# V rows of the second token half gathered as 32 tokens of four experts, multiplied in four column groups of TensorE

## What is computed

```python
def peer_ffn(xn, w_query, sub_keys, expert_u, expert_v):
    ...                       # q, scores, top 16 of each half, top 16 of the pairs
    expert_idx = jnp.take_along_axis(cand_i, best_pos, axis=-1)   # 8 x 16 experts per token
    gates = jax.nn.softmax(best_s, axis=-1)
    def chunk_fn(args):
        xb, ib, gb = args
        u = expert_u[ib]
        act = jax.nn.gelu(jnp.einsum('ced,cd->ce', u, xb))
        return jnp.einsum('ce,ced->cd', gb * act, expert_v[ib])
```

## Time and profile before

| | us |
|---|---|
| median of 3 runs | 2021.76 (2018.59 to 2022.65) |
| the profiled execution, its own time | 2023.32 |
| its span in the trace | 2021.6 |
| mean granted clock of TensorE | 0.97 |

### The profile page before, as it was taken

The page is one execution under the profiler, slowest core; times in us unless marked ns, Lnnn a source line. Parts: engine busy times, 40 slices in busy tenths (PEclk is TensorE's granted clock), DMA queues, the critical chain, the costliest instruction groups (busy, mean ns, idle before and its releaser), DMA issues.

```text
span 2021.6 us, 23901 instructions
## 1 busy us (share of the span) xinstructions
PE 1925.9 (95%) x9007; PEld 1244.1 (62%) x9007; DVE 1166.8 (58%) x2908; ACT 446.2 (22%) x1045; POOL 871.3 (43%) x786
## 2 busy tenths in 40 slices
PE   8999999999989999999998889999999989999998
PEld 7688886856866888885766766444445543333332
DVE  1022111002968888788889999877768764533321
ACT  2233211121202454221211354000013321111112
POOL 0000000000756433545657455645557776656643
PEclk9999999999989999999999678999999989999999
DMA  7533454433999977999899687999999999999997
GB/s 245 151 115 113 146 157 147 146 104 125 365 333 390 315 257 245 365 385 384 325 361 380 227 275 246 403 409 409 409 385 369 368 376 410 409 409 409 409 370 291
DMA packets 252440, 613.48 MB, mean 303 GB/s; under 512 B 18677, under 2 KB 121125, under 8 KB 252325
## 3 DMA queue, kind: packets, MB, share of 16 engines
q0 software_dynamic: 110592, 402.70, 52.7%
q1 hardware_dynamic: 141120, 208.17, 29.8%
q10 hardware_dynamic: 612, 1.07, 0.2%
HBM read 609.77 MB, written 2.10 MB: 303 GB/s over the span
## 4 chain that ended last, share of the span: by engine, by line
PE 68%; DMA 15%; DVE 9%; POOL 4%; issue 2%; ACT 1%; SPq 0%; ACTq 0%; DVEq 0%; POOLq 0%
PE ps L620 27%; PE ps L899 11%; PE ps L849 9%; DMA u_rows<-in_peer_u_dram,idx 8%; PE ps L635 7%; DVE u_rows L1398 4%; PE ps L889 3%; PE ps L662 3%; DMA v_rows<-in_peer_v_dram,idx_turned 3%; DMA wring<-in_w_in_dram 2%; POOL u_rows L579 2%; POOL v_rows L593 2%; DMA wring<-in_peer_w_query_dram 1%; PE ps L649 1%; PE ps L688 1%
## 5 line engine op out<-in xcount | busy, mean ns | idle before, releaser
L579 POOL DMA_INDIRECT u_rows<-in_peer_u_dram,idx x512 | 589.1, 1151 | 971.7 <-DVE idx L1384 505.0
L1398 DVE CUSTOM_DVE_ANT_0 u_rows<-u_rows,xn 128x1024 f32<-128x1024 f32 x512 | 621.0, 1217 | 171.1 <-DMA u_rows<-in_peer_u_dram,idx 167.8
L620 PE MATMUL ps<-xT,wring 128*128 128x256 f32 x2432 | 553.0, 386 | 25.5 <-DMA wring<-in_peer_w_query_dram 11.7
L620 PEld LDWEIGHTS ps<-xT,wring 128*128 128x128 f32 x2432 | 462.8, 193 | 94.5 <-DMA wring<-in_peer_w_query_dram 13.3
L899 PE MATMUL ps<-d_rows,gates 128*128 128x512 f32 x1024 | 456.3, 599 | 0.0
L899 PEld LDWEIGHTS ps<-d_rows,gates 128*128 128x128 f32 x1024 | 190.2, 190 | 266.0 <-issue 265.2
L849 PE MATMUL ps<-v_rows,diag 64*64 64x512 f32 x1928 | 247.0, 631 | 18.1 <-DMA v_rows<-in_peer_v_dram,idx_turned 18.1
L593 POOL DMA_INDIRECT v_rows<-in_peer_v_dram,idx x121 | 131.9, 1090 | 115.1 <-PE ps L849 92.7
L889 PEld LDWEIGHTS ps<-hot_b,hot_a 128*128 128x128 f32 x1024 | 142.7, 224 | 50.5 <-issue 33.5
L1094 ACT ACTIVATE diag<-ident,wgt 128x64 f32<-128x64 f32 x256 | 76.1, 336 | 426.4 <-PE ps L849 415.8
L889 PE MATMUL ps<-hot_b,hot_a 128*128 128x64 f32 x1024 | 150.1, 311 | 15.8 <-DVE hot_b L1465 11.1
(11 more groups left out here) (202 smaller groups left out, 1713.5 us busy)
## 6 DMA issues: line engine op xcount, KB each, us to landing
wring<-in_w_in_dram SPq DMA_DIRECT2D x128, 512.0 KB, 5.0
d_rows<-in_peer_v_dram SPq DMA_DIRECT2D x128, 512.0 KB, 6.8
wring<-in_peer_w_query_dram SPq DMA_DIRECT2D x32, 512.0 KB, 9.0
wring<-in_w_branch_conv_dram SPq DMA_DIRECT2D x16, 512.0 KB, 4.5
wring<-in_w_branch_attn_dram SPq DMA_DIRECT2D x16, 512.0 KB, 5.3
wring<-in_w_out_dram SPq DMA_DIRECT2D x16, 512.0 KB, 4.7
wring<-in_xattn_wq_dram SPq DMA_DIRECT2D x16, 512.0 KB, 4.8
wring<-in_xattn_wo_dram SPq DMA_DIRECT2D x16, 512.0 KB, 5.6
```

The source lines that it names most:

```text
L579: pool.indirect_dma_start(out=u_rows[:, n % URING, :], out_offset=None, in_=peer_u[0], in_offset=bass.IndirectOffsetOnAxis(ap=experts_of(g ...
L620: mm = pe.matmul(bank(job)[:, 0:HN], w[:, k % 4, P * b:P * (b + 1)], act[:, k, :], start=(k == 0), stop=(k == KT - 1))
L1398: dve.tensor_tensor_reduce(out=u, in0=u, in1=(xn2 if h else xn1)[:, i, :], scale=1.0, scalar=0.0, op0=ALU.mult, op1=ALU.add, accum_out=dot ...
```

## The change

1. A V gather now brings 32 tokens of four experts. With m = 16 g + 4 s + b, the partition 32 q + p holds the row of expert 4 q + s of token 32 b + p. `expert_quad` works four gathers: for each bank four matmuls, b = 0 to 3, each with 128 rows of the array and 32 of its columns, so each gather's sum lands in PSUM partitions 32 b to 32 b + 31. That is 8 matmuls for four gathers where there were 16.
2. The expert numbers and weights are spread over the partitions by ScalarE: `spread_experts` and `spread_weights`, 16 copies each for a group. VectorE's copies to `idx_turned` go, and its three writes of the weights become one. The identity is 32 wide and stacked four times (GpSimd, three additions once).
3. One bank pair for each tile of tokens: `add_experts` adds once for each tile, and the wait of the second tile for the first tile's addition goes.
4. Rings: `DRING` 8 to 12; `v_rows` 6 places, 8 from gather 51 on, 10 from gather 202 on. Places come free by fours (`v_used` counts quads).
5. The tables of positions: the first chunks begin at slot 256+16 instead of 256+12, the second ones run over 28 slots from 155 in place of 26 from 151. V gathers by slot (counted from 256): 27 instead of 22 ahead of slot 48, 58 instead of 36 ahead of 150, 142 instead of 120 ahead of 178, 238 instead of 230 ahead of 256. `PLACES` moves the units of the front of half 1 by -2 to +8 slots, most by 3 or 4 later, the last from 254 to 255.
6. `keep_running` ahead of the transposes: 0, 4 and 4 matmuls instead of 4, 12 and 4. One addition in `select` is a tensor_tensor in place of a tensor_scalar.

```diff
-    URING, VRING, DRING, GRING, IRING = 8, 8, 8, 4, 8
+    URING, VRING, DRING, GRING, IRING = 8, 10, 12, 4, 8
+    BLOCK = P // 4
-    CH_SLOT = spread(12, 46, 32) + spread(151, 177, 32)
+    CH_SLOT = spread(16, 46, 32) + spread(155, 179, 32)
-    V_SLOT = (spread(24, 46, 22) + spread(48, 150, 14) + spread(151, 177, 84) + spread(179, 256, 110)
-              + spread(256, 280, 26))
+    V_SLOT = (spread(24, 46, 26) + spread(46, 80, 13) + spread(80, 115, 14) + spread(115, 150, 5) + spread(150, 178, 84) + spread(178, 210, 28) + spread(210, 240, 35) + spread(240, 256, 33) + spread(256, 268, 13) + spread(268, 280, 5))
+    WEIGHTS_AT = [HSTEPS + TOPK * (g + 1) + 8 for g in range(HG)]
-        DIAG_OF.setdefault(slot + (DIAG_BEHIND if slot >= STEPS - 16 else -DIAG_AHEAD), []).append(m)
-        if m % 2:
-            PAIR_OF.setdefault(slot, []).append(m - 1)
+        DIAG_OF.setdefault(max(slot + (DIAG_BEHIND if slot >= STEPS - 16 else -DIAG_AHEAD), WEIGHTS_AT[m // TOPK]),
+                           []).append(m)
+        if m % 4 == 3:
+            QUAD_OF.setdefault(slot, []).append(m - 3)
...
-            eng.wait_ge(v_used, m // 2 + 1)
+            eng.wait_ge(v_used, m // 4 + 1)
...
-            def expert_pair(m):
+            def expert_quad(m):
                 if m == 0:
                     pe.wait_ge(wt_done, 2 * SBH)
-                if m == HSTEPS // 2:
-                    pe.wait_ge(hadd, 2)
-                pe.wait_ge(diag_rdy, m + 2)
-                for k in (m, m + 1):
-                    wait_row(pe, k)
-                first, last = m % (HSTEPS // 2) == 0, m % (HSTEPS // 2) == HSTEPS // 2 - 2
+                tile, n = m // (HSTEPS // 2), m % (HSTEPS // 2)
+                pe.wait_ge(diag_rdy, m + 4)
+                for b in range(4):
+                    wait_row(pe, m + b)
                 for c in range(2):
-                    for k, turn in ((m, 0), (m + 1, 64)):
-                        for r in (0, 64):
-                            o = (r + turn) % P
-                            mm = pe.matmul(ps[o:o + 64, 2 * (r // 64) + c, :], diag[r:r + 64, k % DRING, :],
-                                           v_row(k)[r:r + 64, BANK * c:BANK * (c + 1)],
-                                           start=first, stop=last)
+                    for b in range(4):
+                        mm = pe.matmul(ps[BLOCK * b:BLOCK * (b + 1), 2 * tile + c, :], diag[:, (m + b) % DRING, :],
+                                       v_row(m + b)[:, BANK * c:BANK * (c + 1)],
+                                       start=(n == 0), stop=(n == HSTEPS // 2 - 4))
                 mm.then_inc(v_used, 1)
...
-                keep_running(4)
+
...
-                keep_running(12)
+                keep_running(4)
...
+            def spread_experts(g):
+                act.wait_ge(idx_rdy, HG + g + 1)
+                for b in range(4):
+                    for q in range(4):
+                        to = idx_quad[BLOCK * q:BLOCK * (q + 1), g, :].rearrange("p (s b) -> p s b", b=4)[:, :, b]
+                        qi = act.activation(to, idx2[BLOCK * b:BLOCK * (b + 1), g, 4 * q:4 * (q + 1)], ACT.Copy)
+                qi.then_inc(quad_idx, 1)
+
+            def spread_weights(g):
+                act.wait_ge(wgt_rdy, HG + g + 1)
+                for b in range(4):
+                    for q in range(4):
+                        to = wgt[BLOCK * q:BLOCK * (q + 1), g, :].rearrange("p (s b) -> p s b", b=4)[:, :, b]
+                        qw = act.activation(to, gl[BLOCK * b:BLOCK * (b + 1), 3, 4 * q:4 * (q + 1)], ACT.Copy)
+                qw.then_inc(quad_wgt, 1)
...
             def add_experts(i):
-                dve.wait_ge(v_used, HSTEPS // 4 * (i + 1))
+                dve.wait_ge(v_used, HSTEPS // 8 * (i + 1))
                 hh = hbuf[:, HT + i, :]
-                for r in range(2):
-                    if r:
-                        dve.wait_ge(hadd, 2 * i + 1)
-                    dve.tensor_tensor(hh, ps[:, 2 * r:2 * r + 2, :].rearrange("p c n -> p (c n)"), hh,
-                                      ALU.add).then_inc(hadd, 1)
+                dve.tensor_tensor(hh, ps[:, 2 * i:2 * i + 2, :].rearrange("p c n -> p (c n)"), hh,
+                                  ALU.add).then_inc(hadd, 1)
```

More of the change, by code:

```diff
@@ L200, in build_trunk @@
     for m in range(HSTEPS):
-        if m == V_LATE:
-            ring = [("v", n, None) for n in (6, 7)] + ring
+        if m in V_GROWS:
+            ring = [("v", 6 + 2 * V_GROWS[m] + n, None) for n in range(2)] + ring
         if m == V_LAST:
@@ L214, in chain_of @@
         return g // 2 if g < HG else g - HG // 2
-    PLACES = [20, 21, 25, 29, 33, 37, 40, 44, 49, 52, 59, 60, 60, 62, 64, 65, 65, 65, 65, 67, 68, 68, 68, 68, 68, 68,
[12 rows of a table removed]
+    PLACES = [20, 21, 25, 29, 32, 36, 39, 43, 48, 50, 57, 58, 58, 61, 63, 64, 64, 64, 64, 67, 68, 68, 68, 68, 68, 68,
[12 rows of a table added]
     SLOT = dict(zip(FRONT[1], PLACES))
@@ L384, in build_trunk @@
         idx_rdy = sem("idx_rdy")
-        turned = sem("turned")
+        quad_idx = sem("quad_idx")
+        quad_wgt = sem("quad_wgt")
         gate_rdy = sem("gate_rdy")
@@ L570, in _ @@
                     wait_job(pool, JOB[("xo", 1, 1)] + 1)
-                    pool.tensor_tensor(ident64[:, :], ident[:, 0:P // 2], ident[:, P // 2:P],
+                    pool.tensor_tensor(ident32[:, :], ident[:, 0:BLOCK], ident[:, BLOCK:2 * BLOCK],
                                        ALU.add).then_inc(iotas, 1)
+                    for q in (2, 3):
+                        pool.wait_ge(iotas, q + 1)
+                        pool.tensor_tensor(ident32[:, :], ident32[:, :], ident[:, BLOCK * q:BLOCK * (q + 1)],
+                                           ALU.add).then_inc(iotas, 1)
                 if n < STEPS:
@@ L590, in _ @@
                     if e == 0:
-                        pool.wait_ge(turned, 2 * (g + 1))
-                    own = idx_turned[:, g, e // 2:e // 2 + 1] if e % 2 else idx2[:, g, e:e + 1]
+                        pool.wait_ge(quad_idx, g + 1)
                     pool.indirect_dma_start(
                         out=v_row(m), out_offset=None, in_=peer_v[0],
-                        in_offset=bass.IndirectOffsetOnAxis(ap=own, axis=0)
+                        in_offset=bass.IndirectOffsetOnAxis(ap=idx_quad[:, g, e:e + 1], axis=0)
                     ).then_inc((v_ready if kind == "v" else u_ready)[place], 16)
@@ L910, in _ @@
                     table_transposes()
-                for m in PAIR_OF.get(tau, []):
-                    expert_pair(m)
+                for m in QUAD_OF.get(tau, []):
+                    expert_quad(m)
                 for ch in range(CHUNKS):
@@ L1088, in diagonal @@
                 if e == 0:
-                    act.wait_ge(wgt_rdy, HG + g + 1)
+                    act.wait_ge(quad_wgt, g + 1)
                 if m == 0:
-                    act.wait_ge(iotas, 3)
+                    act.wait_ge(iotas, 5)
                 if m >= DRING:
-                    act.wait_ge(v_used, (m - DRING) // 2 + 1)
-                act.activation(diag[:, m % DRING, :], ident64[:, :], ACT.Copy,
+                    act.wait_ge(v_used, (m - DRING) // 4 + 1)
+                act.activation(diag[:, m % DRING, :], ident32[:, :], ACT.Copy,
                                scale=wgt[:, g, e:e + 1]).then_inc(diag_rdy, 1)
@@ L1151, in _ @@
                     take_tables()
+                if tau + TOPK - 4 in WEIGHTS_AT:
+                    spread_experts(WEIGHTS_AT.index(tau + TOPK - 4))
+                if tau in WEIGHTS_AT:
+                    spread_weights(WEIGHTS_AT.index(tau))
                 for m in DIAG_OF.get(tau, []):
@@ L1337, in select @@
                                   top_v[:, 1, 0:near].unsqueeze(1).to_broadcast([P, TOPK, near]), ALU.add)
-                t0 = after(dve.tensor_scalar(rest_of_first, top_v[:, 1, near:TOPK], top_v[:, 0, 0:1], None, ALU.add))
+                t0 = after(dve.tensor_tensor(rest_of_first, top_v[:, 1, near:TOPK],
+                                             top_v[:, 0, 0:1].to_broadcast([P, near]), ALU.add))
                 yield
@@ L1385, in select @@
                                          op0=ALU.mult, op1=ALU.add).then_inc(idx_rdy, 1)
-                if h:
-                    yield
-                    dve.wait_ge(idx_rdy, g + 1)
-                    odd = idx2[:, g - HG, :].rearrange("p (e two) -> p e two", two=2)[:, :, 1]
-                    for r in (0, 64):
-                        dve.tensor_copy(idx_turned[64 - r:P - r, g - HG, :], odd[r:r + 64, :]).then_inc(turned, 1)
             def dot(n):
@@ L1439, in gelu @@
                     else:
-                        for odd, p0, turn in ((0, slice(0, P), 0), (1, slice(0, 64), 64), (1, slice(64, P), -64)):
-                            to, a3, a2 = (t[:, k, :].rearrange("p (e two) -> p e two", two=2)[:, :, odd]
-                                          for t, k in ((wgt, g - HG), (s3, 0), (s2, 0)))
```

(6 more changed lines are left out.)

15 lines of the change are left out of this document (9 added, 6 removed), and 24 rows, old and new, of the table PLACES.

## The result

The changed kernel is slower by 0.34%: its ratio to the kernel before is 1.0034, 95% interval [1.0022, 1.0045], from 22 executions of each (medians 2032.03 and 2024.59 us). The forecast was 0.8% faster, and its range ended at 2026. The profiled execution took 2030.03 us, its span 2028.3.

A forecast was written before the change was run, and what follows sets the result against it. Transfers at the 409 GB/s ceiling and TensorE both filled B and D; after the change transfers alone would bind. Terms -6.4 - 3.7 + 3 - 8 - 1.2 = -16.3 us took 2023.3 to 2007.0, stated as median 2006, range 1986 to 2026.

The forecast's parts named there:

- the term of C: Second chunks with most V gathers, 1500 to 1660 us: ring freed by fours costs +3 us, within 0 to 19.
- rival 2: TensorE's clock falls in second-chunk stretch, or ring of fours reaches its upper bound: 2015 to 2040 us; 17%.
- V matmuls: TensorE's V work: 64 quads at 1.95 us replace 128 pairs at 1.95, saving 125 us of TensorE's time.
- Rivals 3 and 4: V quads: weight loads laid bare, 4.16 us each, 2024, 6%; or column tiles taking turns, 6.9 us, about 2180, 4%.
- rival 4: V quads: the four column tiles take turns, 6.9 us a quad, about 2180 us in total; 4%.
- B: First 64 dense blocks, 1265 to 1495 us: bound by transfers; 17 more objects make it 22 us longer.
- D and tail: Second 64 blocks with V gathers, from 1665 us to the end: bound by transfers, 22 fewer objects, -28 us.
- slower issues: Tail: the last gathers go at 1.40 instead of 1.28 us, giving 2 us back; together -8 us.
- A: First 32 chunks, 1125 to 1250 us: VectorE's 2.74 us wait and turned copies go, -3.7 us.
- ScalarE: 512 small spreading copies, 108 us, lie in ScalarE's idle time: 0 us on the total.
- The units of the front moved by `PLACES`: Front of half 1, units moved by up to 8 slots: 0 us, bounds 10 us to either side.
- The -0.8%: Whole kernel: forecast median 2006 us, 0.8% less; the forecast itself, 1997 to 2014, had 50%.

The follow-up runs named there:

- c1: The kernel before, unchanged, traced on the same chip as three other kernels as their reference; ratio 1.
- c2: The changed kernel itself as a control, against the kernel before on the same chip; ratio 1.0033 [1.0016, 1.0050].
- e5: Changed kernel with quads between slots 148 and 178 worked and freed as two halves; ratio to before 0.9980 [0.9964, 0.9996].
- e6: Changed kernel with four more V-row places, borrowed from the dense blocks' ring from slot 150 to 174; ratio to before 0.9982 [0.9958, 1.0007].
- c4: Changed kernel with halves, quads aligned to the entry and borrowed places, against the kernel before on the same chip; ratio 0.9925 [0.9899, 0.9951].
- e3: Kernel before, pairs and slots kept, but places for V gathers freed by fours; ratio to before 1.0063 [1.0041, 1.0084].
- e7: Changed kernel with V_SLOT, CH_SLOT and PLACES of the kernel before; ratio to before 1.0049 [1.0028, 1.0071].
- e1: Changed kernel with its second chunks at the old slots, 26 from 151; ratio to before 1.0026 [1.0004, 1.0049].
- c3: Changed kernel with three unread matmuls behind each first-tile V quad from slot 148, against before on the same chip; ratio 1.0044 [1.0022, 1.0066].
- e2: Changed kernel with four unread matmuls ahead of each first-tile V quad from slot 148 on; ratio to before 1.0070 [1.0046, 1.0095].
- e10: Changed kernel with halves between slots 148 and 178, first chunks and unread matmuls as before the change; ratio to before 0.9992 [0.9969, 1.0015].
- e12: Changed kernel with halves, quads aligned to the entry, places borrowed from the stretch's ninth V gather on; ratio to before 0.9914 [0.9884, 0.9945].

## Why the prediction was wrong

**The step that failed is the term of C.** I took +3 us within bounds of 0 to 19. It was 26.3 us in the first pair of traces and 17.7 in the second, and without it the change would have been a gain. The mechanism behind the bounds was right: GpSimd, with every U gather behind it, waits for places of a ring that comes free by fours. Its waits for TensorE in C went from 15.2 to 39.5 us (17.6 to 34.5 in c1 and c2); e5 and e6 lowered them and gave some 15 us back by freeing finer or by more places, and c4 left 4.9 us of them and no loss. What was mis-sized is the value inside the bounds, taken near the lower one because few quads were to have a chunk in the way:

- The bounds counted a quad at 1.95 us. The 21 quads of C took 61.9 us, 2.9 each. With 2.9 the same sum reaches 29 us instead of 19.
- The ring of fours by itself cost 5 to 9 us of C (e3, e7). The other 12 to 17 came with the new tables of positions, whose effect on C I had at nothing. Putting the chunks back alone did not recover them (e1); whether it was the V slots or `PLACES` was not separated, and stays open.
- I read 8.4 us of waits in C from a window that began at 1500 us. It left out the 6.85 us ahead of the gather of 1498.72; from slot 150 on they were 15.2. Of the ring's wait at the entry the sum therefore knew nothing. It did not grow by more than 1 us, but it was there to be removed, and c4 did that.

The measured 2032 lies in the 2015 to 2040 of rival 2, which held "the ring of fours at its upper bound" in one case with the clock, at 17%.

**Rival 2's clock.** It fell as described, to 0.76 in C. It is not needed for the cure: e6 gave C back 15 us at a clock of 0.79. That it has no share of its own is not shown. In c3 the quads took 51.9 us instead of 61.3, and GpSimd's waits did not fall with them (40.3 us against 34.5); but 46.8 us of unread matmuls came into TensorE's order, and where it worked through without a gap, as from 1563 to 1614 us, each three of them put chunk and quad off by 2.7 us. e2 has the same flaw ahead of the quads.

**V matmuls: right.** 1.92 to 1.93 us a quad at full clock, 3.6 at the low one; busy 163.9 us instead of 125, as many ran at the low one. Rivals 3 and 4 fell: four tiles that share all rows hide their weight loads too. How rival 4 comes to an estimate of 2.5 us is not shown (6.9 / 2.38 is 2.9); neither would have changed the sum.

**Transfers bound B and D: right.** 17 objects more made B 22.7 us longer (24.9 in c2 against c1; 22 forecast), so the cheaper matmuls bought nothing there. D and tail, -42 and -43 against -37. The end of the changed kernel in order of time, for the earlier trace rows:

```profile
2002.94 0.93 POOL L600 DMA_INDIRECT v_rows<-in_peer_v_dram,idx_quad  x1 [0.30 <-issue]
2004.17 0.94 POOL L600 DMA_INDIRECT v_rows<-in_peer_v_dram,idx_quad  x1 [0.31 <-issue]
2005.42 0.94 POOL L600 DMA_INDIRECT v_rows<-in_peer_v_dram,idx_quad  x1 [0.30 <-issue]
...
2020.90 1.23 DVE L1487 TENSOR_TENSOR hbuf<-ps,hbuf 128x1024 f32<-128x1024 f32 x1 [5.15 <-PE ps L852]
```

The last gathers go out 1.24 us apart without a wait, where before 5.54 us lay ahead of one of them, and one addition of 1.23 us is left of two. I had taken 0.12 us off for each of them as slower issues, and that was not needed.

**A: wrong by 5 to 7 us, in part a matter of where A begins.** VectorE's wait of 2.74 us for the table is gone, but slots 0 to 48 took 162.7 and 160.2 us in two traces of the changed kernel and 159.5 and 158.4 in two of before. The changed kernel around its transposes, for the earlier trace rows:

```profile
1112.28 3.60 PE L860 MATMUL ps<-xn,ident 128*128 128x512 f32 x8
1129.00 1.33 PE L892 MATMUL ps<-hot_b,hot_a 128*128 128x64 f32 x5 [13.12 <-DVE hot_b L1480]
```

TensorE stands idle for 13.1 us before its first chunk, and VectorE's waits for TensorE's chunks in A came to 9.9 us instead of 3.0. e10, with chunks and unread matmuls as before, did not mend A. The same work scatters from 158 to 172 us over the traces. Where A was longest, the stretch ahead of it was short: in e1 and e6 171.7 us behind 1092.2 and 1090.8, and in e6 VectorE waited 12.4 us at 1100 to 1113 us for work that hung on the last units of the front. The front's end reaches into A, so the first two lines of the table are better taken together: -0.7 us, and -3.1 in c2 against c1, where -3.7 was forecast.

The ring of six places freed by fours is not the cause. In A it raised GpSimd's waits for TensorE from 2.7 us to 18.8 in e3 and 27.0 in e7, and A stayed at 160.0 and 158.4. In the kernel before, GpSimd waited 59.4 us of A for VectorE; there it had the time to give, which in C it had not.

**ScalarE: right.** The page's lines of the copies, weights and experts:

```profile
L1102 ACT ACTIVATE wgt<-gl 32x4 f32<-32x4 f32 x256 | 52.9, 206 | 111.9 <-DVE gl L1460 109.1
...
L1094 ACT ACTIVATE idx_quad<-idx 32x4 uint32<-32x4 uint32 x256 | 52.7, 206 | 2.9
```

512 at 0.206 us, 105.6 us where 108 was forecast. In the whole of A VectorE waited 5.0 us for ScalarE, before 7.0, so the copies stayed hidden. The units of the front moved by `PLACES` cost nothing either: the start to slot 0 came out 3.9 and 4.9 us shorter, within the 10 us to either side that I gave them.

**The -0.8%.** c4 measured 0.9925 and e12 0.9914, near the forecast. Part of this is luck: its terms are not those of the forecast. In the traces, C is 4.4 us shorter than in c1 where +3 was forecast, A 10.5 us longer where -3.7 was, and D with the tail 40.1 us shorter where 37 was.

## What to carry to other kernels

When transfers fill a stretch, a cheaper matmul there only moves work; ask what its new unit of release does to whoever issues the transfers. In a ring freed k places at a time, up to k - 1 places can be held by rows of a unit whose last row is still on its way, and one queue that stands still for a place holds every gather behind it. That costs where this queue sets the pace (C) and nothing where it has time to give (A). Check it where the rate steps up, with the landing time of the full queue (medians of 16 to 18 us in B) and not that of the free one (6). Where TensorE has time to spare, half the parallelism and a release twice as fine was the better kernel (e5).

## What the runs showed of the hardware

Four matmuls of 128 rows by 32 columns, in float32 and each with its own rows streaming, ran side by side: 16 instructions of 512 columns in 1.93 us, the time of 16 in four 64x64 tiles, with nothing to be seen of their weight loads of 0.130 us each between them. The Trainium skill ("TensorE: Matmul & The Clock Gate", Part 3) says that weight loads overlap matmuls in flight only where the row groups differ. The runs show otherwise: the four tiles share all rows, and a quad stays at 1.93 us.

GpSimd's gathers of 128 rows of 4 KB go out 1.24 to 1.4 us apart when nothing holds them, about as dense as the ceiling of 409 GB/s takes them (1.28 us). In C, where no other queue moved much, its waits left 326 GB/s of it in the changed kernel and 374 in c4.
